# A grouped state-space recurrence: making the read matrices on GpSimd instead of VectorE

## The chip, the cores and the metric

One core of one Trainium2 chip. The metric is the device time of one launch of the whole kernel in microseconds. The kernel before takes 4410.57 us (median of 3 runs, 4408.84 to 4411.85).

## What is computed

Two transformer-like blocks over 256 tokens of width 2048, all in float32. The change touches one stage of the second block, the diagonal state-space layer of `layer_c`. Cut to what matters:

```python
def s5_ssm(u, lam_re, lam_im, log_step, b_re, b_im, c_re, c_im, d):
    """Groups of 16 channels share a 64-dim complex diagonal state.
    x_t = Lbar x_{t-1} + Bbar u_t ; y_t = Re(C x_t) + D u_t."""
    ...
    bu_re = jnp.einsum('gpc,blgc->blgp', bb_re, uf)
    bu_im = jnp.einsum('gpc,blgc->blgp', bb_im, uf)
    ...
    _, _, x_re, x_im = lax.associative_scan(_complex_combine, (a_re, a_im, bu_re, bu_im), axis=1)
    y = (jnp.einsum('gcp,blgp->blgc', c_re.astype(f32), x_re)
         - jnp.einsum('gcp,blgp->blgc', c_im.astype(f32), x_im))
    return y.reshape(Bsz, L, E) + d.astype(f32) * uf.reshape(Bsz, L, E)

def layer_c(x, ...):
    u, gate = jnp.split(h @ w_in, 2, axis=-1)
    y = s5_ssm(u, ...).astype(x.dtype)
    z = jax.nn.gelu(y)
    z = z * jax.nn.sigmoid(z @ glu_w + glu_b)
    return x + (z * jax.nn.silu(gate)) @ w_out
```

## The kernel before

The kernel is a row of stages with a barrier behind each. The stage in question is `s5_blocks` (line 1910), between the GEMM stage that makes `u` and the GEMM stage `glu`. Its 128 groups of channels are taken as 64 pairs (two groups of 64 states fill 128 partitions), and the 64 pairs in four batches `q` = 0 to 3 of 16 pairs (`QP`). Time is cut into steps of 4 tokens (`STEP`), and the 64 steps into 8 rows by 8 columns (`ROWS`, `COLS`). For each batch these pieces are made; the names are those of the functions in `s5_blocks`:

- **drive matrices** (GpSimd, lines 1962 to 1977). From the raw B coefficients (`ss_raw`) and a table of powers (`s_drive`): twice (real and imaginary part) a product into `ss_p`, a second product, and the sum or difference of both into `ss_drive_t`, in two halves of 64 partitions. 8 instructions a batch. `ss_drive_t` has one buffer, so batch q + 1 waits until TensorE has done `kernels(q)` (the wait on `within`, line 1966).
- **turn(q)** (TensorE) transposes them, ScalarE copies them out (`take_g`); **states(q)** multiplies them with `u`, ScalarE copies the result to `ss_x` (`take_x`).
- **read matrices** `read_rows(q)` (VectorE, lines 2105 to 2119). The same form from the raw C coefficients and the table `s_read`, for STEP + 1 = 5 powers: 8 instructions a batch, through `ss_b` into `ss_read`, which has two buffers. Its end counts up `h_done`, for which `kernels(q)` waits (line 2002). The SP queue's load of the raw coefficients of batch q + 2 waits for `gt_done` and `h_done` of batch q.
- **scan(q)** (VectorE, lines 2127 to 2139): the walk over the states in place in `ss_x`. 7 x 4 instructions of 128x256, one copy, 6 x 4 of 128x32, 7 x 4 of 128x256: 81 instructions, each waiting for the one before (`link`), then `scanned` counts up.
- **skip(q)** (VectorE, line 2144): one small product for the term D u; it waits for `kernels(q-1)`.
- **kernels(q)** (TensorE, lines 2009 and 2011): the matrices inside a step, from `ss_read` and `ss_drive_t`; ScalarE copies them to `ss_within` (`take_m`).
- **outputs(q)** (TensorE, lines 2023 and 2025): needs `take_m(q)` and `scan(q)` (line 2016); ScalarE puts the GELU of it into `c_ug` (`put`).

The orders are written by hand. TensorE: turn(0), states(0), kernels(0), then for each q: turn(q+1), states(q+1), outputs(q), kernels(q+1). ScalarE: take_u, take_g, take_x, take_m of batch q + 1, then put(q). VectorE: memsets of `ss_read`, `ss_within` and `ss_x`, skip(0), read_rows(0), then for each q: scan(q), skip(q+1), read_rows(q+1). GpSimd: a memset of `ss_drive_t`, then the drive matrices of the four batches.

Of the kernel before, what the change touches and what calls it, by code (L numbers as in the profile page):

```python
# [18 lines left out]
ALU = mybir.AluOpType  # L19
# [3 lines left out]
P = 128  # L23
# [1768 lines left out]
STEP = 4  # L1792
NQ = 4
QP = PAIRS // NQ
# [115 lines left out]
def s5_blocks(st, nc, t, banks, u, tables, con):  # L1910
# [3 lines left out]
    with ExitStack() as own, st.stage() as (block, sem):  # L1914
        def sb(name, shape):
            return own.enter_context(nc.sbuf_tensor("ss_" + name, shape, F32))

        drive, read, leaps = tables
        leap, leap_swing = leaps[:, ::2], leaps[:, 1:]
        C = 16  # L1920
        raw = sb("raw", [P, 2, QP, 4, C])
# [3 lines left out]
        h = sb("read", [P, 2, QP, 2, STEP + 1, 32])  # L1925
# [3 lines left out]
        b1, b2 = sb("b1", [P, QP, STEP + 1, C]), sb("b2", [P, QP, STEP + 1, C])  # L1929
# [3 lines left out]
        raw_in = [sem("ss_raw_in0"), sem("ss_raw_in1")]  # L1933
        d_in, cleared, zeroed, chain, gchain = sem("ss_d_in"), sem("ss_cleared"), sem("ss_zeroed"), sem("ss_chain"), sem("ss_gchain")
        gt_done, turned, g_out = sem("ss_gt_done"), sem("ss_turned"), sem("ss_g_out")
        h_done, within, m_out = sem("ss_h_done"), sem("ss_within"), sem("ss_m_out")
        stacked, driven, x_in = sem("ss_stacked"), sem("ss_driven"), sem("ss_x_in")
        scanned, y_done, z_out, d_done = sem("ss_scanned"), sem("ss_y_done"), sem("ss_z_out"), sem("ss_d_done")
        own_group = [(slice(64 * k, 64 * k + 64), slice(C * k, C * k + C)) for k in range(2)]
        stack = [(r, s) for r in range(4) for s in range(STEP)]  # L1940

        def pairs(q):
            return slice(q * QP, (q + 1) * QP)
# [4 lines left out]
        @block.sync  # L1948
        def _(sp):
            sp.dma_start(dcol[:, :], t["s5_d"]).then_inc(d_in, 16)  # L1950
            for q in range(NQ):
                if q >= 2:
                    sp.wait_ge(gt_done, 2 * (q - 1))
                    sp.wait_ge(h_done, 2 * (q - 1))
                sp.dma_start(raw[:, q % 2, :, :, :], t["s5_bc"][:, pairs(q), :, :]).then_inc(raw_in[q % 2], 16)

        @block.gpsimd
        def _(gp):
            link = Chain(gp, gchain)
            nc.gpsimd.memset(gt[:, :, :, :, :], 0.0).then_inc(cleared, 1)  # L1960
            gp.wait_ge(cleared, 1)
            for q in range(NQ):
                gp.wait_ge(raw_in[q % 2], 16 * (q // 2 + 1))
                if q >= 1:
                    gp.wait_ge(turned, 8 * q)
                    gp.wait_ge(within, 4 * q)
                row = lambda k: raw[:, q % 2, :, k, :].unsqueeze(2).broadcast_to([P, QP, STEP, C])
                by = lambda k: drive[:, k, :, pairs(q)].rearrange("p s q -> p q s").unsqueeze(3).broadcast_to([P, QP, STEP, C])
                for part, ((a, b), (c, d), op) in enumerate((((0, 0), (1, 1), ALU.subtract), ((0, 1), (1, 0), ALU.add))):
                    link(nc.gpsimd.tensor_tensor(p1[:, :, :, :], row(a), by(b), ALU.mult))  # L1970
                    link(nc.gpsimd.tensor_tensor(p2[:, :, :, :], row(c), by(d), ALU.mult))
                    for n, (rows, cols) in enumerate(own_group):
                        ins = nc.gpsimd.tensor_tensor(gt[rows, :, part, :, cols], p1[rows, :, :, :], p2[rows, :, :, :], op)
                        if n == 0:
                            link(ins)
                    ins.then_inc(gt_done, 1)
                    gp.wait_ge(gt_done, 2 * q + part + 1)

        @block.tensor
        def _(pe):  # L1980
# [115 lines left out]
        @block.vector  # L2096
        def _(dve):
            link = Chain(dve, chain)
            nc.vector.memset(h[:, :, :, :, :, :], 0.0).then_inc(zeroed, 1)
            nc.vector.memset(m[:, :, :, :], 0.0).then_inc(zeroed, 1)  # L2100
            nc.vector.memset(x[:, :, 0, :, :, 0], 0.0).then_inc(zeroed, 1)
            dve.wait_ge(d_in, 16)
            dve.wait_ge(zeroed, 3)

            def read_rows(q):
                dve.wait_ge(raw_in[q % 2], 16 * (q // 2 + 1))
                if q >= 2:
                    dve.wait_ge(y_done, 2 * (q - 1))
                row = lambda k: raw[:, q % 2, :, k, :].unsqueeze(2).broadcast_to([P, QP, STEP + 1, C])
                by = lambda k: read[:, k, :, pairs(q)].rearrange("p s q -> p q s").unsqueeze(3).broadcast_to([P, QP, STEP + 1, C])  # L2110
                for part, ((a, b), (c, d), op) in enumerate((((2, 0), (3, 1), ALU.subtract), ((2, 2), (3, 3), ALU.add))):
                    link(nc.vector.tensor_tensor(b1[:, :, :, :], row(a), by(b), ALU.mult))
                    link(nc.vector.tensor_tensor(b2[:, :, :, :], row(c), by(d), ALU.mult))
                    for n, (rows, cols) in enumerate(own_group):
                        ins = nc.vector.tensor_tensor(h[rows, q % 2, :, part, :, cols], b1[rows, :, :, :], b2[rows, :, :, :], op)
                        if n == 0:
                            link(ins)
                    ins.then_inc(h_done, 1)
                    dve.wait_ge(h_done, 2 * q + part + 1)

            def advance(out, previous, a, b, t1, t2):
                link(nc.vector.tensor_tensor(t1, previous, a, ALU.mult))
                link(nc.vector.tensor_tensor(t2, previous[:, ::-1], b, ALU.mult))
                link(nc.vector.tensor_tensor(t1, t1, t2, ALU.add))
                link(nc.vector.tensor_tensor(out, out, t1, ALU.add))

            def scan(q):
                xs = x[:, q % 2]
                dve.wait_ge(x_in, 4 * (q + 1))
                wide = lambda k: (leap[:, 0:1, k, pairs(q)].unsqueeze(3).broadcast_to([P, 2, QP, COLS]), leap_swing[:, :, k, pairs(q)].unsqueeze(3).broadcast_to([P, 2, QP, COLS]))  # L2130
                for i in range(1, ROWS):
                    advance(xs[:, i + 1], xs[:, i], *wide(0), m1[:, :, :, :], m2[:, :, :, :])
                link(nc.vector.tensor_copy(xs[:, 0, :, :, 1:], xs[:, ROWS, :, :, 0:COLS - 1]))
                for b in range(2, COLS):
                    advance(xs[:, 0, :, :, b], xs[:, 0, :, :, b - 1], leap[:, 0:1, ROWS - 1, pairs(q)].broadcast_to([P, 2, QP]), leap_swing[:, :, ROWS - 1, pairs(q)],
                            m1[:, :, :, 0], m2[:, :, :, 0])
                for i in range(1, ROWS):
                    advance(xs[:, i], xs[:, 0], *wide(i - 1), m1[:, :, :, :], m2[:, :, :, :])
                dve.sem_inc(scanned, 1)

            def skip(q):
                if q >= 1:
                    dve.wait_ge(within, 4 * q)
                nc.vector.tensor_tensor(diag[:, :, :], con["ident"][0:32, 0:32].unsqueeze(1).broadcast_to([32, QP, 32]),
                                        dcol[:, pairs(q)].unsqueeze(2).broadcast_to([32, QP, 32]), ALU.mult).then_inc(d_done, 1)

            skip(0)
            read_rows(0)
            for q in range(NQ):
                scan(q)  # L2150
                if q + 1 < NQ:
                    skip(q + 1)
                    read_rows(q + 1)


def layer_c(st, nc, t, banks, con, xT):

    with ExitStack() as own:
# [8 lines left out]
        with ExitStack() as s1:  # L2167
# [5 lines left out]
            def gate_out(act, f, psum, link):  # L2173
# [4 lines left out]
                dict(kind="fm", n=16, cols=T, rhs=lambda s, k: h[s][:, k, :], evac=gate_out)], gemm_buffers(sb, "c", s1, slots=2), banks,  # L2178
                operand=(h4, *h, quarters()))
        s5_blocks(st, nc, t, banks, ug[:, 0:KT, :], tables, con)  # L2180
        s5.close()
        buffers = gemm_buffers(sb, "c2", own)
# [322 lines left out]
```

## Time and profile before

| what | value |
|---|---|
| median of 3 runs | 4410.57 us |
| the profiled execution's own time | 4413.94 us |
| its span, first to last instruction | 4412.3 us |
| the stage s5_blocks in it | 3869.97 to 4170.06 us, 300.09 us |
| in the stage: PE, DVE, ACT, POOL busy | 183.45, 229.53, 148.02, 87.62 us |
| in the stage: mean granted TensorE clock | 0.69 |
| over the whole span: PE, DVE, ACT, POOL busy | 78%, 60%, 14%, 21% |

Instructions are named by their engine (PE is TensorE, PEld its weight loads, DVE VectorE, ACT ScalarE, POOL GpSimd) and by the line of the kernel. Busy times of a stretch say how much of it each engine worked; the granted clock is 1.00 at TensorE's full speed of 2.4 GHz and 0.50 at 1.2 GHz. Times in the rows are microseconds from the span's start.

### The profile page before, as it was taken

How to read it: one execution, taken by the hardware profiler on the slowest of the kernel's cores; microseconds unless marked ns; L12 is line 12 of the kernel's file. 1: busy time of each engine (PE TensorE's matmuls, PEld its weight loads, DVE VectorE, ACT ScalarE, POOL GpSimd, SP SyncE). 2: the span in 40 equal slices, each digit the busy share in tenths (PEclk: the TensorE clock that was granted, in tenths of full speed). 3: DMA queues.
4: the chain of work that ended last, by engine and by line, in shares of the span. 5: the costliest groups of instructions: out<-in, count | busy, mean ns of one | idle time of the engine just before them, and what ended most of it. 6: DMA issues, size and time to landing. Idle time of an engine off the chain costs nothing. (4 is left out here: it accounts for less than half of the span.)

```text
span 4412.3 us, 46250 instructions
## 1 busy us (share of the span) xinstructions
PE 3423.7 (78%) x17280; PEld 2498.0 (57%) x17280; DVE 2660.3 (60%) x3168; ACT 635.7 (14%) x1310; POOL 942.3 (21%) x753
## 2 busy tenths in 40 slices
PE   6899993776988755777778777779996687956688
PEld 1688671546988752333323333239874486944588
DVE  6774226657976567656566565426655466678665
ACT  0200002321100101111111111010003200134400
POOL 0100003002100016554545545300002000033040
PEclk9899895788989878999999999989996598976699
DMA  8573210025944439999999999935540033400143
GB/s 331 222 270 133 95 57 9 2 77 213 367 158 171 143 152 415 421 422 422 422 422 422 422 422 422 422 133 205 186 141 11 28 134 133 171 15 5 58 152 114
DMA packets 137329, 940.09 MB, mean 213 GB/s; under 512 B 17514, under 2 KB 22890, under 8 KB 24075
## 3 DMA queue, kind: packets, MB, share of 16 engines
q0 software_dynamic: 82944, 604.02, 33.5%
q1 hardware_dynamic: 54292, 334.89, 21.1%
q8 instruction: 52, 0.85, 0.1%
q14 instruction: 41, 0.34, 0.0%
HBM read 936.75 MB, written 2.10 MB: 213 GB/s over the span
## 5 line engine op out<-in xcount | busy, mean ns | idle before, releaser
L1313 PE MATMUL bank<-pe_v_rows,pe_diag 128*128 128x512 f32 x2048 | 959.8, 618 | 357.4 <-DMA pe_v_rows<-in_expert_v,pe_staged_v 215.2
L1313 PEld LDWEIGHTS bank<-pe_v_rows,pe_diag 128*128 128x128 f32 x2048 | 385.2, 196 | 931.4 <-issue 519.2
L1211 DVE SCALAR_TENSOR_TENSOR pe_junk<-pe_u_rows,h_rows 128x2048 f32<-128x2048 f32 x256 | 586.9, 2293 | 460.0 <-DMA pe_u_rows<-in_expert_u,pe_staged_u 448.9
L1155 POOL DMA_INDIRECT pe_v_rows<-in_expert_v,pe_staged_v x256 | 317.6, 1240 | 376.6 <-PE bank L1313 312.9
L1155 POOL DMA_INDIRECT pe_u_rows<-in_expert_u,pe_staged_u x256 | 338.0, 1320 | 228.3 <-DVE pe_junk L1211 134.4
L169 PE MATMUL bank<-h_top,b_top 128*128 128x256 f32 x1024 | 292.9, 286 | 40.2 <-DVE b_rest L237 40.2
L169 PE MATMUL bank<-h_rest,b_top 128*128 128x256 f32 x1024 | 292.3, 285 | 0.0
L169 PE MATMUL bank<-h_top,b_rest 128*128 128x256 f32 x1024 | 292.2, 285 | 0.0
L169 PEld LDWEIGHTS bank<-h_top,b_top 128*128 128x128 f32 x1024 | 199.4, 195 | 40.8 <-DVE b_rest L237 40.8
L1281 ACT ACTIVATE pe_diag<-ident,pe_weights 128x128 f32<-128x128 f32 x256 | 97.7, 399 | 786.9 <-PE bank L1313 786.5
L169 PEld LDWEIGHTS bank<-h_rest,b_top 128*128 128x128 f32 x1024 | 199.3, 195 | 0.0
L169 PEld LDWEIGHTS bank<-h_top,b_rest 128*128 128x128 f32 x1024 | 199.2, 195 | 0.0
L235 DVE CAST in_top<-in_ring 128x2048 fp32r<-128x2048 f32 x48 | 58.8, 1224 | 219.6 <-PE bank L195 134.6
L169 PE MATMUL bank<-h_top,in_top 128*128 128x256 f32 (+1 forms) x512 | 173.3, 339 | 11.2 <-DVE in_rest L237 11.2
L169 PE MATMUL bank<-h_rest,in_top 128*128 128x256 f32 (+1 forms) x512 | 173.1, 338 | 0.0
L169 PE MATMUL bank<-h_top,in_rest 128*128 128x256 f32 (+1 forms) x512 | 173.1, 338 | 0.0
L169 PE MATMUL bank<-gelu_top,c_top 128*128 128x256 f32 x512 | 147.3, 288 | 31.8 <-DVE c_rest L237 31.8
L169 PE MATMUL bank<-h_top,c_top 128*128 128x256 f32 x512 | 146.2, 286 | 20.8 <-DVE c_rest L237 20.8
L235 DVE CAST c_top<-c_ring 128x2048 fp32r<-128x2048 f32 x64 | 78.5, 1226 | 128.2 <-PE bank L169 128.2
L237 DVE TENSOR_TENSOR c_rest<-c_ring,c_top 128x2048 fp32r<-128x2048 f32 x64 | 150.9, 2358 | 2.2
L237 DVE TENSOR_TENSOR b_rest<-b_ring,b_top 128x2048 fp32r<-128x2048 f32 x64 | 146.7, 2292 | 2.2
L169 PE MATMUL bank<-gelu_rest,c_top 128*128 128x256 f32 x512 | 146.9, 287 | 0.0
(486 smaller groups left out, 7427.8 us busy)
## 6 DMA issues: line engine op xcount, KB each, us to landing
ab_ring<-in_w_ab SPq DMA_DIRECT2D x56, 1024.0 KB, 4.8
in_ring<-in_w_in_a SPq DMA_DIRECT2D x48, 1024.0 KB, 4.9
mod_ring<-in_w_mod SPq DMA_DIRECT2D x32, 1024.0 KB, 7.2
v_rows<-in_w_mod POOLq DMA_DIRECT2D x32, 1024.0 KB, 5.2
b_ring<-in_w_in_gates SPq DMA_DIRECT2D x32, 1024.0 KB, 5.2
k_cols<-in_w_mod POOLq DMA_DIRECT2D x32, 1024.0 KB, 5.3
c_ring<-in_w_c_in SPq DMA_DIRECT2D x32, 1024.0 KB, 4.8
b_ring<-in_w_branches SPq DMA_DIRECT2D x16, 1024.0 KB, 4.8
```

Of the source, the lines that this page charges most:

```text
L169: mm = nc.tensor.matmul(banks[s][:, half * n:(half + 1) * n], fast(weights), fast(seg["rhs"](b, k)), start=(j == 0 and m == 0), stop=(j == ...
L235: nc.vector.tensor_copy(fast(top[:, s % 2, :]), ring[:, s % slots, :]).then_inc(topped, 1)
L237: nc.vector.tensor_tensor(fast(rest[:, s % 2, :]), ring[:, s % slots, :], top[:, s % 2, :], ALU.subtract).then_inc(split_done, 1)
L1155: gp.indirect_dma_start(buf[:, slot, :], None, table, bass.IndirectOffsetOnAxis(ap=staged[which][:, tile, e:e + 1], axis=0)).then_inc(sems ...
L1211: nc.vector.scalar_tensor_tensor(out=junk[:, :], in0=ub[:, s, :], scalar=1.0, in1=h2tm[:, tile, :], op0=ALU.mult, op1=ALU.mult, accum_out= ...
L1281: nc.scalar.activation(diag[:, e % 4, :], con["ident"], ACT.Copy, scale=wts[:, tile, e:e + 1]).then_inc(diag_done, 1)
L1313: mm = nc.tensor.matmul(banks[4 * tile + b][:, :], diag[:, e % 4, :], vb[:, s, b * 512:(b + 1) * 512], start=False, stop=False, skip_group ...
```

## The change

Function `read_rows` moves from VectorE's program to GpSimd's, word for word but for the engine. GpSimd runs it for batch q right behind the drive matrices of batch q; its wait for VectorE's memsets (`zeroed`), which VectorE itself had, is made once, at q = 0. VectorE keeps the memsets, skip and scan. No size, buffer, load or semaphore count changes, and the programs of TensorE, ScalarE and the SP queue stay as they are. In the changed kernel the lines from here on have numbers that are 2 to 20 higher.

```diff
@@ GpSimd's program
             gp.wait_ge(cleared, 1)
+
+            def read_rows(q):
+                gp.wait_ge(raw_in[q % 2], 16 * (q // 2 + 1))
+                if q == 0:
+                    gp.wait_ge(zeroed, 3)
+                if q >= 2:
+                    gp.wait_ge(y_done, 2 * (q - 1))
+                row = lambda k: raw[:, q % 2, :, k, :].unsqueeze(2).broadcast_to([P, QP, STEP + 1, C])
+                by = lambda k: read[:, k, :, pairs(q)].rearrange("p s q -> p q s").unsqueeze(3).broadcast_to([P, QP, STEP + 1, C])
+                for part, ((a, b), (c, d), op) in enumerate((((2, 0), (3, 1), ALU.subtract), ((2, 2), (3, 3), ALU.add))):
+                    link(nc.gpsimd.tensor_tensor(b1[:, :, :, :], row(a), by(b), ALU.mult))
+                    link(nc.gpsimd.tensor_tensor(b2[:, :, :, :], row(c), by(d), ALU.mult))
+                    for n, (rows, cols) in enumerate(own_group):
+                        ins = nc.gpsimd.tensor_tensor(h[rows, q % 2, :, part, :, cols], b1[rows, :, :, :], b2[rows, :, :, :], op)
+                        if n == 0:
+                            link(ins)
+                    ins.then_inc(h_done, 1)
+                    gp.wait_ge(h_done, 2 * q + part + 1)
+
             for q in range(NQ):
                 gp.wait_ge(raw_in[q % 2], 16 * (q // 2 + 1))
...
                     ins.then_inc(gt_done, 1)
                     gp.wait_ge(gt_done, 2 * q + part + 1)
+                read_rows(q)
@@ VectorE's program
-            def read_rows(q):
...
             skip(0)
-            read_rows(0)
             for q in range(NQ):
                 scan(q)
                 if q + 1 < NQ:
                     skip(q + 1)
-                    read_rows(q + 1)
```

GpSimd's order of work from the first batch on, of the kernel before (`ss_drive_t` are the drive matrices; a batch is two such groups of three rows, and `x2` the two halves):

```order
L1960 MEMSET ss_drive_t 128x4096
L1970 TENSOR_TENSOR ss_p<-ss_raw,s_drive 128x1024
L1971 TENSOR_TENSOR ss_p<-ss_raw,s_drive 128x1024
L1973 TENSOR_TENSOR ss_drive_t<-ss_p 64x16x4x16 x2
L1970 TENSOR_TENSOR ss_p<-ss_raw,s_drive 128x1024
L1971 TENSOR_TENSOR ss_p<-ss_raw,s_drive 128x1024
L1973 TENSOR_TENSOR ss_drive_t<-ss_p 64x16x4x16 x2
L1970 TENSOR_TENSOR ss_p<-ss_raw,s_drive 128x1024
```

The same place of the changed kernel (lines 1989 to 1992 are the drive matrices there, 1972 to 1975 the read matrices):

```order
L1989 TENSOR_TENSOR ss_p<-ss_raw,s_drive 128x1024
L1990 TENSOR_TENSOR ss_p<-ss_raw,s_drive 128x1024
L1992 TENSOR_TENSOR ss_drive_t<-ss_p 64x16x4x16 x2
L1972 TENSOR_TENSOR ss_b<-ss_raw,s_read 128x1280
L1973 TENSOR_TENSOR ss_b<-ss_raw,s_read 128x1280
L1975 TENSOR_TENSOR ss_read<-ss_b 64x16x5x16 x2
L1972 TENSOR_TENSOR ss_b<-ss_raw,s_read 128x1280
L1973 TENSOR_TENSOR ss_b<-ss_raw,s_read 128x1280
L1975 TENSOR_TENSOR ss_read<-ss_b 64x16x5x16 x2
L1989 TENSOR_TENSOR ss_p<-ss_raw,s_drive 128x1024
```

Between the drive matrices of two batches, 8 instructions of 1280 elements a partition now stand in GpSimd's queue.

VectorE's order at the end of a scan, of the kernel before:

```order
L2125 TENSOR_TENSOR ss_x<-ss_x,ss_m 128x256
L2144 TENSOR_TENSOR ss_skip<-ident,ss_d 32x512
L2112 TENSOR_TENSOR ss_b<-ss_raw,s_read 128x1280
L2113 TENSOR_TENSOR ss_b<-ss_raw,s_read 128x1280
L2115 TENSOR_TENSOR ss_read<-ss_b 64x16x5x16 x2
```

and of the changed kernel:

```order
L2129 TENSOR_TENSOR ss_x<-ss_x,ss_m 128x256
L2148 TENSOR_TENSOR ss_skip<-ident,ss_d 32x512
L2126 TENSOR_TENSOR ss_m<-ss_x,s_leaps 128x256
L2127 TENSOR_TENSOR ss_m<-ss_x,s_leaps 128x256
L2128 TENSOR_TENSOR ss_m<-ss_m 128x256
```

The next scan follows right behind skip.

## Rows read from the trace of the kernel before

**Rows 1.** Busy time by engine, the whole stage (us, count; then clock, DMA share, GB/s)

```profile
3869.97:4170.06 300.09, 183.45 (x1152) 145.54 (x1152) 229.53 (x363) 148.02 (x321) 87.62 (x33) 0.69 0.02 8
```

**Rows 2.** Waits in the stage: who waited for whom, us, times, longest

```profile
POOL ss_p L1970 <- PE bank L2011: 128.5, 3, 61.8
...
PE bank L1987 <- POOL ss_drive_t L1973: 93.0, 4, 27.9
```

**Rows 3.** Timeline of TensorE: start, us, work, count, idle time before it

```profile
3943.48 1.75 PE L1987 MATMUL bank<-ident,ss_drive_t 128*128 128x128 f32 x7 [18.21 <-POOL ss_drive_t L1973]
...
3960.13 0.41 PE L2023 MATMUL bank<-ss_u,ss_within 128*128 128x64 f32 x2 [3.09 <-DVEq L2139]
...
3980.16 1.06 PE L2009 MATMUL bank<-ss_read,ss_drive_t 128*32 128x128 f32 x4
...
4046.03 0.39 PE L2023 MATMUL bank<-ss_u,ss_within 128*128 128x64 f32 x2
...
4056.85 0.62 PE L2009 MATMUL bank<-ss_read,ss_drive_t 128*32 128x128 f32 x4
...
4109.29 0.39 PE L2023 MATMUL bank<-ss_u,ss_within 128*128 128x64 f32 x2
...
4142.84 0.66 PE L2023 MATMUL bank<-ss_u,ss_within 128*128 128x64 f32 x2 [8.51 <-ACT c_ug L2082]
```

**Rows 4.** Busy time by engine, three stretches of outputs and kernels (clock behind POOL's)

```profile
3960.13:4005.10 44.97, 44.95 (x192) 31.37 (x192) 41.71 (x90) 5.11 (x12) 0.00 (x0) 0.51 0.04 12
4046.03:4071.10 25.07, 25.05 (x194) 18.56 (x193) 21.95 (x64) 5.77 (x14) 0.00 (x0) 1.00 0.01 1
4142.84:4163.00 20.16, 20.16 (x95) 20.16 (x95) 0.00 (x0) 12.15 (x32) 0.00 (x0) 0.50 0.00 1
```

**Rows 5.** Timeline of GpSimd, drive matrices of three batches

```profile
3875.09 2.01 POOL L1970 TENSOR_TENSOR ss_p<-ss_raw,s_drive 128x1024 f32<-128x1024 f32 x1 [1.63 <-DMA ss_raw<-in_s_bc]
...
3925.45 2.01 POOL L1970 TENSOR_TENSOR ss_p<-ss_raw,s_drive 128x1024 f32<-128x1024 f32 x1 [28.40 <-PE bank L2011]
...
3929.63 4.78 POOL L1973 TENSOR_TENSOR ss_drive_t<-ss_p 64x1024 f32<-64x1024 f32 x2
...
4071.25 2.30 POOL L1970 TENSOR_TENSOR ss_p<-ss_raw,s_drive 128x1024 f32<-128x1024 f32 x1 [38.30 <-PE bank L2011]
4073.63 2.07 POOL L1971 TENSOR_TENSOR ss_p<-ss_raw,s_drive 128x1024 f32<-128x1024 f32 x1
4075.78 4.88 POOL L1973 TENSOR_TENSOR ss_drive_t<-ss_p 64x1024 f32<-64x1024 f32 x2
```

**Rows 6.** Timeline of VectorE, parts of three scans

```profile
3929.66 2.40 DVE L2122 TENSOR_TENSOR ss_m<-ss_x,s_leaps 128x32 f32<-128x32 f32 x1
...
3972.86 0.42 DVE L2122 TENSOR_TENSOR ss_m<-ss_x,s_leaps 128x256 f32<-128x256 f32 x1
...
3985.70 0.28 DVE L2133 COPY ss_x<-ss_x 128x224 f32<-128x224 f32 x1
...
3992.04 0.43 DVE L2122 TENSOR_TENSOR ss_m<-ss_x,s_leaps 128x256 f32<-128x256 f32 x1
...
4073.86 2.12 DVE L2123 TENSOR_TENSOR ss_m<-ss_x,s_leaps 128x256 f32<-128x256 f32 x1
4076.02 2.45 DVE L2124 TENSOR_TENSOR ss_m<-ss_m 128x256 f32<-128x256 f32 x1
...
4110.25 0.43 DVE L2122 TENSOR_TENSOR ss_m<-ss_x,s_leaps 128x256 f32<-128x256 f32 x1 [3.45 <-ACT ss_x L2063]
```

**Rows 7.** Timeline of VectorE, half of the read matrices of a batch

```profile
4094.67 1.47 DVE L2112 TENSOR_TENSOR ss_b<-ss_raw,s_read 128x1280 f32<-128x1280 f32 x1
...
4097.70 3.01 DVE L2115 TENSOR_TENSOR ss_read<-ss_b 64x1280 f32<-64x1280 f32 x2
```

**Rows 8.** Timeline of GpSimd, dense two-input products elsewhere in the kernel

```profile
1021.95 6.42 POOL L990 TENSOR_TENSOR o_a<-o_a,mo_wa 128x2048 f32<-128x2048 f32 x1
...
3500.14 4.51 POOL L1724 TENSOR_TENSOR ab_of<-ab_of,ab_gates 128x2048 f32<-128x2048 f32 x1 [99.15 <-POOLq L51]
```

More of the change, by code:

```diff
@@ L2103, in _ @@
             dve.wait_ge(zeroed, 3)
-            def read_rows(q):
[L2106 to L2119, printed above, removed]
             def advance(out, previous, a, b, t1, t2):
```

## Prediction

> **What bounds the kernel now.** The change touches one stage of 300.09 us, so I read that stretch by itself. First the busy times [rows 1]: no engine is full; VectorE works 229.53 us of it, TensorE 183.45, GpSimd only 87.62. Going by shares, moving work from VectorE to GpSimd looks right. The waits say something else [rows 2]: GpSimd waits 128.5 us in all for TensorE's kernels, and TensorE waits 93.0 us for GpSimd's drive matrices. The stage is a ring: kernels(q) end, drive matrices(q+1), turn and states(q+1), outputs(q), kernels(q+1). I call the end of kernels(q) K(q). Before, K(0) is 3925.3 (GpSimd starts again at 3925.45 [rows 5]), K(1) 4005.1, K(2) 4071.1 [rows 4].
>
> Two things disturb the ring. **The clock** [rows 3, 4]: outputs and kernels took 25.07 us where they followed states at once (granted clock 1.00), and 44.97 us after a pause of 3.09 us (0.51). After a pause of 8.51 us outputs alone took 20.2 us at 0.50, against 4056.85 - 4046.03 = 10.8. Slow kernels alone are 4005.10 - 3980.16 = 24.9 us. 1.00 is 2.4 GHz and 0.50 is 1.2. **VectorE and GpSimd block each other**: a walk instruction of 128x256 takes 0.46 us from start to start (28 of them and nothing else fill 3972.86 to 3985.70), but while drive matrices are made it takes 2.12 or 2.45 us, as long as the GpSimd instruction beside it (2.07, and 4.88 for two); even one of 128x32 takes 2.40 us [rows 5, 6]. So while GpSimd works through two-input instructions, VectorE gets one of its own in for each. GpSimd hardly suffers: 2.07 against 2.01.
>
> **What is moved, and its price.** VectorE gives up 8 instructions a batch, half a batch from 4094.67 to 4100.7 [rows 7], 12.1 us a batch. GpSimd gains them. It has no such instruction of 1280 elements; the nearest are its own drive instructions of 1024 in the same layout. Two products and their gaps are 4.18 us, two halves 4.86 with the gap [rows 5], so drive matrices take 2 x 9.04 = 18.1 us. Scaled by 1280/1024, half a batch of read matrices is 5.2 + 6.1 = 11.3 and a batch 22.6 us. Bounds: below, no growth with size, 18.1; above, the dense products of 2048 elements, 4.51 us (2.8 for 1280), and far off 6.42 (4.0) [rows 8], up to some 33 us a batch. I take 22.6, the same form.
> - Where does it lie? Behind the drive matrices, beside turn and states. GpSimd's chain for a batch is now 18.1 + 22.6 = 40.7 us from K(q), some 42 when VectorE takes turns with it. TensorE needs 18.8 + 13.6 (turn and states, 3943.48 to 3957.04) + 10.8 (outputs) = 43.2 before it wants `ss_read`. From batch 1 on read matrices are on time.
> - The cost is on scan(q). It needs 3 parts: 12.8 + 6.3 + 12.8 = 32 us alone [rows 6]. It now meets 16 GpSimd instructions a batch instead of 8, and moves 16 steps of its 81 in those 42 us.
> - Waits added on GpSimd: `zeroed` is long there, `y_done` is two batches old. The load of the raw coefficients leaves later but is needed a batch later; nothing. The 8 matching waits go from VectorE; its skip is 0.7 us as before.
>
> The Trainium skill, page SBUF — State Buffer, section "two separate sides", calls the shared ports an exclusive lock held for the whole instruction, the loser fully blocked. The rows agree on VectorE's side; on GpSimd's, 2.07 against 2.01 with a 0.42 us instruction between says most of that one is hidden. By the rule each GpSimd instruction in contention would be 0.4 us longer, and the sum some 6 us more (16 of them in scan(1)'s way).
>
> **The walk.** Drive(0) starts at 3875.09 and is no longer disturbed by read rows on VectorE: it ends at 3875.09 + 18.1 + 0.2 for skip(0) = 3893.4. States(0) end at 3907.0. Read(0) ends at 3916.0, so kernels(0) start after a pause of 9.0 us, at half clock like the 8.51 us pause: K(0) = 3916.0 + 24.9 = 3940.9, 15.6 later than before. Scan(0) starts 1 us behind states [rows 3, 6], at 3908.0. It gets 3 steps in until 3916.0, then 24.9 us free: 25 large, the copy, 24 small, 15 large. 13 are left at K(0): 8 beside drive(1), 5 beside read(1), done at K(0) + 18.9 + 14.2 = 33.1. States(1) end at K(0) + 32.5. No pause worth the name, so outputs(0) and kernels(1) run fast: K(1) = K(0) + 58.2 = 3999.1. Before it was 79.8: this turn gains 21.6.
>
> Scan(1) starts at K(0) + 33.9, does 3 steps until 42.0 and in the free 16.2 us about 43; 35 are left at K(1). 16 go by until K(1) + 42.0, 19 more in 8.7: done at 50.7. States(2) end at K(1) + 38.2, as now from K(2) to 4109.29 (ScalarE is first busy with put and take_u). TensorE pauses 12.5 us and outputs(1) and kernels(2) run at half clock, 45.0: K(2) = K(1) + 95.8 = 4094.9, against 66.0 before. Scan(2) then finds GpSimd idle and is done before K(2), so the third turn stays at 63. Scan(3) starts at about K(2) + 39 as before, with one or two of its steps held up by the end of read(3), and what follows stays: 0 to 1.5 us. Sum against the profiled execution: +15.6 - 21.6 + 29.8 + 0.7 = **+24.5 us**, all in this stage. That execution took 4413.94 by its own time; the median of the runs is 4410.57, 0.08% below. Forecast 4410.57 + 24.5 = **4435**. A difference of 0.2%, 8.8 us, is about what a measurement of this kernel can tell from none.
>
> **Rivals.**
> - *One step more in scan(0)* (chance 0.17). The tie of 33.1 against 32.5 is the walk's weakest place. One more blocked step, 3 us, makes a pause like the 3.09 us one: outputs(0), kernels(1) slow, K(1) = K(0) + 81. Then scan(1) is in time (K(2) = K(1) + 63.3 = 4085.2), scan(2) ends at K(2) + 45.2, K(3) comes 90.3 behind K(2), and the last outputs follow at half clock, 35.5 us (8 for the first half of put(2), 20.2, and 7 from 4163.0 to 4170.06 as now): end at 4211, +41, 4451.
> - *GpSimd's instructions nearer the dense bound* (0.10): 2.8 and 3.3 us instead of 2.5 and 3.0. Read(0) ends 2.6 later and each contended scan pays again: 4446; at 4.0 us about +60.
> - *The clock comes back while TensorE works* (0.11). K(0) = 3930.3; scan(0) ends at K(0) + 53, K(1) near 4008.4, K(2) 4075.3, scan(3) at K(2) + 74.6. With fast last outputs the end is 1.5 us before today's, with slow ones 7 behind: 4409 to 4418. Against it: 45 us of busy TensorE in [rows 4] at 0.51. The Trainium skill, TensorE: Matmul & The Clock Gate, Part 1, has sustained activity release the throttle; by that rule this is the case. Here transposes got the clock back and outputs and kernels did not.
> - *Faster: the ring gains because scans keep up* (0.06). If GpSimd's 1280 instructions cost no more than those of 1024 (read batch 18.1 us), or the two engines did not block each other, scan(1) ends by K(1) + 40, too little pause for the clock to fall: K(1) 3993 to 3998, K(2) near 4060, then 99 us: end 10 to 13 before today's, 4398 to 4401. It decides where a read batch is under about 20 us. For it: VectorE does lose 12.1 us a batch. Against it: [rows 5, 6].
>
> **The numbers.** The forecast case has 0.56, with small variations of 4 to 5 us in K(0) and scan(1). Faster 0.06, same 0.11 (the clock rival), slower 0.83. The range 4412 to 4452 holds the forecast case, the tie rival, the upper part of the clock rival and most of the dense one; left out are the faster case, the low edge of the clock rival and the far bound of GpSimd's price, under 2 in 10.
>
> **What would show it.** Read instructions on GpSimd near 2.5 and 3.0 us; VectorE's walk instructions of 2 to 3 us beside them, some 16 a batch; kernels(0) starting near 3916 after a pause, clock 0.50; K(0) near 3941, K(1) near 3999, K(2) near 4095; outputs(1) waiting for scan(1) by 10 us or more at half clock; the stage about 325 us long. Wrong if walk instructions keep 0.46 us beside the new ones, if the clock returns within kernels(0), or if the stage is not longer than 309 us.

## The result and the profile after

The changed kernel takes 4440.28 us (median of 6 runs, 4432.85 to 4449.17) against 4411.74 (6 runs, 4408.84 to 4415.32) of the kernel before: 1.0066 times as long, 95% interval 1.0053 to 1.0079, +28.5 us. Forecast was 4435, in a range of 4412 to 4452. Run again on another occasion (5 runs, against 13 of the kernel before) it was 4438.82 against 4414.94, 1.0053 times (1.0039 to 1.0067), +23.9.

| | before | after |
|---|---|---|
| the profiled execution's own time | 4413.94 | 4449.17 |
| its span | 4412.3 | 4447.1 |
| stage s5_blocks | 3869.97 to 4170.06, 300.09 | 3881.26 to 4205.10, 323.84 |
| in the stage: PE, DVE, ACT, POOL busy | 183.45, 229.53, 148.02, 87.62 | 196.19, 209.12, 148.21, 162.18 |
| in the stage: granted clock | 0.69 | 0.64 |

The stage grew by 23.75 us; forecast +24.5. In this execution the stages ahead of it, whose code is the same, took another 11.3 us (the stage begins at 3881.26 instead of 3869.97). In the second profiled execution of the same program the stage began at 3862.70, earlier than before, and again took 323.85. So the stage's length belongs to the program, and the 11.3 us ahead of it are scatter of an execution.

Busy time by engine of the changed kernel over the stage, as in [rows 1]:

```profile
3881.26:4205.10 323.84, 196.19 (x1152) 150.96 (x1152) 209.12 (x331) 148.21 (x321) 162.18 (x65) 0.64 0.02 7
```

GpSimd's busy time has nearly doubled. VectorE's fell by only 20 us, although its read instructions had been busy for 66 us before (35.3 + 17.0 + 13.9 in the groups by shape): blocked steps count as busy. The waits in the stage (who waited for whom, us, times, longest), as in [rows 2]:

```profile
POOL ss_p L1989 <- PE bank L2031: 95.9, 3, 55.4
...
PE bank L2007 <- POOL ss_drive_t L1992: 80.1, 4, 24.4
DVE ss_m L2126 <- ACT ss_x L2083: 60.0, 2, 38.5
```

VectorE now waits 60.0 us for the states, 27.1 before: it has time to spare in some batches and none in others. Timeline of TensorE, the first matmuls behind its pauses (idle time in brackets), and outputs(0), which follow states without one:

```profile
3927.03 1.06 PE L2029 MATMUL bank<-ss_read,ss_drive_t 128*32 128x128 f32 x4 [8.19 <-POOL ss_read L1975]
...
3984.20 0.39 PE L2043 MATMUL bank<-ss_u,ss_within 128*128 128x64 f32 x2
...
4059.60 0.66 PE L2043 MATMUL bank<-ss_u,ss_within 128*128 128x64 f32 x2 [10.79 <-issue]
...
4177.88 0.66 PE L2043 MATMUL bank<-ss_u,ss_within 128*128 128x64 f32 x2 [9.38 <-DVEq L2143]
```

Busy times of the four stretches of kernels and outputs that begin there, the clock third from the end:

```profile
3927.03:3952.00 24.97, 24.92 (x96) 11.39 (x96) 22.74 (x66) 5.13 (x13) 0.00 (x0) 0.50 0.07 22
3984.10:4009.30 25.20, 25.15 (x195) 18.66 (x194) 23.73 (x45) 5.79 (x15) 9.64 (x4) 1.00 0.07 22
4059.50:4105.20 45.70, 45.57 (x192) 31.96 (x192) 29.87 (x82) 5.12 (x12) 0.00 (x0) 0.50 0.00 1
4177.88:4198.60 20.72, 20.71 (x96) 20.52 (x96) 0.00 (x0) 11.35 (x30) 0.00 (x0) 0.50 0.00 1
```

Kernels(0) at half clock after a pause of 8.19 us; outputs(0) and kernels(1) at full clock, 25.2 us, where they took 44.97 before [rows 4]; outputs(1) and kernels(2) at half clock, 45.7, after 10.79.

Added up along TensorE, the 23.75 us are these. Half clock adds 41.0 us to what the same matmuls take at 1.00, against 29.7 before: 10.7 in kernels(0), 20.5 in outputs(1) and kernels(2), 9.8 in outputs(3). That is 11.3 more. The pauses ahead of kernels and outputs are 28.4 us, against 11.6: 16.8 more. Turn(0) starts 23.6 us into the stage and not 27.1, 3.6 less, since VectorE's read matrices no longer hold up the drive matrices of batch 0. The rest is 0.8 less.

Timeline of GpSimd from K(0) on, drive matrices and then read matrices (as [rows 5]):

```profile
3952.12 2.22 POOL L1989 TENSOR_TENSOR ss_p<-ss_raw,s_drive 128x1024 f32<-128x1024 f32 x1 [25.15 <-PE bank L2031]
...
3956.57 4.91 POOL L1992 TENSOR_TENSOR ss_drive_t<-ss_p 64x1024 f32<-64x1024 f32 x2
...
3970.83 2.54 POOL L1972 TENSOR_TENSOR ss_b<-ss_raw,s_read 128x1280 f32<-128x1280 f32 x1
...
3976.09 5.99 POOL L1975 TENSOR_TENSOR ss_read<-ss_b 64x1280 f32<-64x1280 f32 x2
```

and of VectorE's walk at the same time (as [rows 6]):

```profile
3952.50 2.12 DVE L2126 TENSOR_TENSOR ss_m<-ss_x,s_leaps 128x256 f32<-128x256 f32 x1
...
3956.81 2.46 DVE L2128 TENSOR_TENSOR ss_m<-ss_m 128x256 f32<-128x256 f32 x1
...
3971.07 2.59 DVE L2126 TENSOR_TENSOR ss_m<-ss_x,s_leaps 128x256 f32<-128x256 f32 x1
...
3976.32 3.00 DVE L2128 TENSOR_TENSOR ss_m<-ss_m 128x256 f32<-128x256 f32 x1
```

Each step lasts about as long as the GpSimd instruction it meets: 2.12 and 2.46 beside drive matrices, 2.59 and 3.00 beside read matrices, against 0.42 alone.

### The profile page after: what moved, and what is told of

It reads as the page before. It is cut to its first block and busy times, and to the rows that moved or that the text cites. A ratio compares the mean times of both kernels' runs of the same rounds, so it can differ in the third digit from the quotient of the medians.

```text
span 4447.1 us, 46248 instructions
## 1 busy us (share of the span) xinstructions
PE 3450.2 (78%) x17280; PEld 2512.5 (56%) x17280; DVE 2640.7 (59%) x3136; ACT 636.0 (14%) x1310; POOL 1028.1 (23%) x785
## 5 line engine op out<-in xcount | busy, mean ns | idle before, releaser
L169 PE MATMUL bank<-h_top,in_top 128*128 128x256 f32 (+1 forms) x512 | 173.2, 338 | 11.3 <-DVE in_rest L237 11.3
```

Source lines behind the costliest of these rows:

```text
L169: mm = nc.tensor.matmul(banks[s][:, half * n:(half + 1) * n], fast(weights), fast(seg["rhs"](b, k)), start=(j == 0 and m == 0), stop=(j == ...
```

## The experiments

Theory A is the prediction's: the two engines block each other, scans come late or in time according to how much free time the batch before left them, and TensorE's clock halves in a pause. Rival B: GpSimd is simply slower, and only matrices that come late cost. Rival C: late scans are the loss, the clock goes along.

**The changed kernel again**, nothing edited.

> The changed kernel once more. Theory A (VectorE's walk steps and GpSimd's two-input instructions block each other, and TensorE's clock halves in the pauses this makes): the stage s5_blocks takes 324 us within 3, with the same four ends of kernels, and the whole kernel 4435 to 4445. In the first profile the stages ahead, whose code is the same, took 11.3 us more than before: if that was scatter of one execution, a new profile shows less of it and the median comes nearer to +24; if it belongs to this program, it comes again.

4438.82 us against 4414.94 before (interval above). The stage took 323.85 us, and the four ends of kernels, counted from the stage's start, are the same within 0.2 us: 70.6, 128.0, 224.0, 287.3. The stages ahead did not repeat their 11 us. The two gaps between medians, +28.5 and +23.9, differ by less than their intervals allow.

**Only batch 0 moved.**

```diff
@@ GpSimd
-                read_rows(q)
+                if q in (0,):
+                    read_rows(q)
@@ VectorE
+                    if q + 1 not in (0,):
+                        read_rows(q + 1)
```

> Only batch 0's read matrices on GpSimd, batches 1 to 3 on VectorE. Theory A: kernels(0) still start late and at half clock (K(0) 15.6 us later than before), which gives scan(0) time to get on, so scan(0) is done when states(1) end, outputs(0) and kernels(1) run at full clock and K(1) = K(0) + 57.6; after that no scan meets read matrices on GpSimd, K(2) = K(1) + 63.3, and the stage ends 9 us EARLIER than before: 4402, between 4399 and 4409. Rival B (GpSimd is just the slower engine, and read matrices that come late are the whole loss): all of the loss is at kernels(0), so this kernel keeps it, +15 us: 4426.

4405.22 us, 0.9976 times the kernel before (0.9966 to 0.9986): faster by 9.7 us. The stage took 291.63 us, 8.5 less. Timeline of TensorE: kernels(0) behind their pause, and outputs(0) without one; and the clock of outputs(0) and kernels(1):

```profile
3913.17 1.06 PE L2030 MATMUL bank<-ss_read,ss_drive_t 128*32 128x128 f32 x4 [8.22 <-POOL ss_read L1975]
...
3970.35 0.39 PE L2044 MATMUL bank<-ss_u,ss_within 128*128 128x64 f32 x2
```

```profile
3970.30:3995.40 25.10, 25.10 (x194) 18.61 (x193) 22.91 (x65) 5.77 (x14) 0.00 (x0) 1.00 0.07 22
```

The late and slow kernels(0) are all there, and the kernel gains. The time they cost is what scan(0) needs to be done before states(1), and 25.1 us at full clock take the place of 44.97. Rival B, which keeps +15 us, falls.

**Only batches 1 to 3 moved.** The same edit with `(1, 2, 3)`; VectorE makes batch 0.

> Batch 0's read matrices on VectorE as before, batches 1 to 3 on GpSimd. Theory A: K(0) as before (3925), but scan(0) has moved only 29 steps by then and needs until K(0) + 57, so outputs(0) and kernels(1) run at half clock, K(1) = K(0) + 102; K(2) = K(1) + 63; scan(2) is late again by 7 us, K(3) = K(2) + 90: the stage ends 46 us later than before, 4457, between 4440 and 4465, slower than the changed kernel although less was moved. Rival B: the matrices of batches 1 to 3 are in time for kernels, so 4412, as before.

4456.25 us, 1.0092 times (1.0076 to 1.0107). Less is moved than in the changed kernel and it is slower. The stage took 344.15 us, 44 more than before (46 worked out). Timeline of TensorE at outputs(0), and the busy times from there:

```profile
3975.90 0.66 PE L2044 MATMUL bank<-ss_u,ss_within 128*128 128x64 f32 x2 [23.29 <-DVEq L2160]
```

```profile
3976.00:4021.00 45.00, 45.00 (x191) 31.87 (x192) 29.75 (x82) 5.11 (x12) 0.00 (x0) 0.50 0.00 1
```

TensorE waited 23.29 us for scan(0), then ran 45 us at half clock. Kernels(1), (2) and (3) followed outputs without a pause, so all read matrices were in time, and rival B's 4412 falls.

**Work that nobody waits for.**

```diff
@@ GpSimd, behind the drive matrices of each batch of the kernel before
+                for part in range(2):
+                    for _ in range(2):
+                        link(nc.gpsimd.tensor_tensor(p1[:, :, :, :], p1[:, :, :, :], p2[:, :, :, :], ALU.subtract))
+                    for rows, cols in own_group:
+                        link(nc.gpsimd.tensor_tensor(p1[rows, :, :, :], p1[rows, :, :, :], p2[rows, :, :, :], ALU.subtract))
```

> The kernel before, with 8 more two-input GpSimd instructions of 1024 elements behind each batch's drive matrices, whose results nobody reads and nobody waits for; GpSimd is idle there. VectorE keeps its read matrices. Theory A: scans lose 8 more of their steps' time per batch and VectorE's chain of a batch gets longer, outputs(0) run late and slow: +20 to +50 us, 4432 to 4462. Rival B (only the matrices' lateness costs): no one waits for these, 4412 within 4.

4462.49 us, 1.0106 times (1.0091 to 1.0122), +47.6, 0.5 us above the upper end of what was expected; the stage took 352.0 us. The new instructions delay no matrix of GpSimd's: ahead of each further batch it still waited for kernels (15.49, 55.43 and 19.09 us). What they hold up is VectorE. Timeline of TensorE at kernels(0) and at outputs(0):

```profile
3907.76 1.06 PE L2014 MATMUL bank<-ss_read,ss_drive_t 128*32 128x128 f32 x4 [1.73 <-DVE ss_read L2120]
...
3980.41 0.66 PE L2028 MATMUL bank<-ss_u,ss_within 128*128 128x64 f32 x2 [15.93 <-DVEq L2144]
```

First VectorE's read matrices of batch 0 come late; kernels(0) run at half clock behind a pause of 1.73 us and end 67.8 us into the stage instead of 55.3. Then scan(0) is late, and TensorE pauses 15.93 us ahead of outputs(0). So the loss is the blocking and the half clock behind it, and rival B falls.

**The pauses filled.**

```diff
@@ TensorE
+            def keep_busy(n):
+                for _ in range(n):
+                    nc.tensor.transpose(banks[0][:, 0:P], con["ident"], con["ident"])
             turn(0)
             states(0)
+            keep_busy(37)
             kernels(0)
...
+                keep_busy((95, 13, 13, 34)[q])
                 outputs(q)
```

> The changed kernel, with transposes of the identity into a bank that nobody reads put where TensorE would pause: 37 ahead of kernels(0), 95 ahead of outputs(0), 13 ahead of outputs(1) and (2), 34 ahead of outputs(3), each about as long as the pause that I work out at full clock. Theory A with the clock as a separate part: kernels(0), outputs and kernels all run at 1.00; scan(0) then meets the read matrices with 42 steps left and ends at K(0) + 53, K(1) = K(0) + 78, K(2) and K(3) 67 apart, stage 299 us within 5, whole kernel 4409 to 4418: most of the change's loss was the half clock. Rival C (lateness of the scans is the loss, the clock only goes along): the stage stays at 320 or more, 4435.

4423.52 us, 1.0025 times (1.0014 to 1.0037), above the 4418 that was the upper end. The profile says why. Timeline of TensorE at kernels(0), of this kernel:

```profile
3900.42 4.21 PE L2051 MATMUL bank<-ident 128*128 128x128 f32 x37
3908.84 0.89 PE L2029 MATMUL bank<-ss_read,ss_drive_t 128*32 128x128 f32 x4 [4.22 <-POOL ss_read L1975]
```

37 transposes lasted 4.21 us, 0.114 each; I had taken 0.21 from those of turn, which wait on ScalarE. A pause of 4.22 us stayed open and kernels(0) took 24.8 us again. The stage took 324.00 us in this execution, no less than in the changed kernel. It was one of the longer ones, 4431.12 us; the ten runs lie between 4417.21 and 4437.47. That the others had fewer stretches at half clock is likely, but not shown, since only this one was profiled. It settles nothing about C, so it was repeated with 72, and 180, 30, 30, 70:

> moved_busy with enough filling: in its trace the transposes went by every 0.114 us, not 0.21, and left half of each pause open (4.2 us ahead of kernels(0)), so that the clock still fell. Now 72 ahead of kernels(0), 180 ahead of outputs(0), 30 ahead of outputs(1) and (2), 70 ahead of outputs(3). Theory A with the clock as a separate part: no kernels or outputs at half clock, K(1) = K(0) + 78, K(2) and K(3) 67 apart, stage 299 us within 6, whole kernel 4410 to 4418. Rival C (late scans are the loss, the clock goes along): 4423 or more.

4414.93 us, 0.9998 times (0.9989 to 1.0007): as the kernel before. Busy times of kernels(0), and of outputs(0) with kernels(1):

```profile
3915.30:3929.60 14.30, 14.22 (x96) 7.80 (x96) 13.10 (x36) 5.15 (x13) 0.00 (x0) 1.00 0.13 38
3982.30:4007.50 25.20, 25.06 (x192) 18.60 (x192) 22.99 (x66) 5.15 (x13) 0.00 (x0) 1.00 0.00 1
```

Both at full clock. The distances of the kernels' ends are 77.9, 67.6 and 66.9 us, worked out 78, 67, 67. The stage took 304.39 us, 19.5 less than the changed kernel's: so much goes when the clock is held, though scan(0) ends later than in either kernel (113 us into the stage; 101 in the changed kernel, 90 before). Rival C as it is stated, 4423 or more, falls. 304.39 stays above the 299 worked out: in the second half of outputs(3) the clock fell all the same (10.05 us, the first half 5.54).

**The same filling in the kernel before**, 14 ahead of outputs(0) and 50 ahead of outputs(3).

> The kernel before, with 14 such transposes ahead of outputs(0) (its pause of 3.09 us) and 50 ahead of outputs(3). Theory A: outputs(0) and kernels(1) take 25 us instead of 45, outputs(3) 11 instead of 21; the later batches shift but stay without pauses; the stage gets 28 us shorter, 272, whole kernel 4387, between 4380 and 4400. Rival C: 4415 as before.

4402.23 us, 0.9973 times (0.9964 to 0.9983), less than half of the gain worked out, in part from the same wrong 0.21 us. The stage took 290.74 us in the profiled execution, one of the longer ones (4408.81; the ten runs lie between 4395.94 and 4409.39). Outputs(0) ran fast, but the pauses were only partly closed and a new one came, since kernels(1) now wait for VectorE's read matrices. Timeline of TensorE, and the busy times behind the second pause:

```profile
3965.14 0.41 PE L2023 MATMUL bank<-ss_u,ss_within 128*128 128x64 f32 x2 [1.70 <-DVEq L2145]
...
3977.89 0.62 PE L2009 MATMUL bank<-ss_read,ss_drive_t 128*32 128x128 f32 x4 [1.85 <-DVE ss_read L2121]
```

```profile
3985.00:4000.00 15.00, 15.00 (x60) 6.81 (x58) 13.50 (x45) 3.44 (x9) 0.00 (x0) 0.50 0.00 0
```

Kernels(1) fell to half clock after pauses of 1.70 and 1.85 us with 11 us of work between. I had not listed this wait: with outputs(0) fast, VectorE's 12.1 us of read matrices stand on the path.

Held clocks shorten both kernels. So these two experiments show that half clock is a cost of its own in each, but not that it is most of what the change costs, as the expectation above says. With transposes in both kernels, the stage is still some 14 us longer with the read matrices on GpSimd (304.39 against 290.74), and neither has its clock held throughout. By the sum along TensorE above, pauses have the larger share.

**The opposite move.**

```diff
@@ VectorE
+            def drive_rows(q):
...
+            drive_rows(0)
             skip(0)
             read_rows(0)
             for q in range(NQ):
                 scan(q)
                 if q + 1 < NQ:
+                    drive_rows(q + 1)
                     skip(q + 1)
                     read_rows(q + 1)
@@ GpSimd: the drive matrices go, two memsets of VectorE's come
+            nc.gpsimd.memset(h[:, :, :, :, :, :], 0.0).then_inc(zeroed, 1)
+            nc.gpsimd.memset(m[:, :, :, :], 0.0).then_inc(zeroed, 1)
```

> The opposite move: VectorE makes the drive matrices too (8 instructions of 1024 elements, 1.25 us each, behind scan(q)), and GpSimd only the memsets of ss_drive_t, ss_read and ss_within. No two-input instruction of GpSimd is left to block VectorE. Theory A: VectorE's instructions all keep their own length (0.42, 1.2, 1.5 us), a batch costs it 32 + 10 + 12 = 54 us, and the stage takes 275 us within 5, whole kernel 4390. Rival B (VectorE is the busiest engine of the stage, 77% by its busy time, and more work on it must lengthen it): 40 us more work, 4440 or so.

4388.15 us, 0.9942 times (0.9926 to 0.9959). The stage took 275.05 us. Timeline of VectorE in this kernel behind scan(0), drive matrices and then read matrices:

```profile
3933.32 1.23 DVE L2094 TENSOR_TENSOR ss_p<-ss_raw,s_drive 128x1024 f32<-128x1024 f32 x1 [0.26 <-DVE ss_x L2123]
...
3935.84 2.47 DVE L2097 TENSOR_TENSOR ss_drive_t<-ss_p 64x1024 f32<-64x1024 f32 x2
...
3943.98 1.47 DVE L2110 TENSOR_TENSOR ss_b<-ss_raw,s_read 128x1280 f32<-128x1280 f32 x1
```

Every instruction keeps its own length. The drive matrices of a batch cost VectorE 10.1 us here. On GpSimd they took 18, in which the walk got only 8 of its steps done, 3.7 us of its work. VectorE has more instructions, is busy for 206.41 us instead of 229.53, since none of them is blocked, and the stage is 25 us shorter. Half of that is at the start: kernels(0) end 43.0 us into the stage instead of 55.3, since the matrices of batch 0 are no longer made by two engines that block each other. The two memsets that go to GpSimd have a part in this, which was not tried by itself. The other half is K(0) to K(1), 67.8 us instead of 79.8, with outputs(0) and kernels(1) at full clock.

**GpSimd with one input.** In the changed kernel, products and sums of the read matrices replaced by copies of the same size.

```diff
-                    link(nc.gpsimd.tensor_tensor(b1[:, :, :, :], row(a), by(b), ALU.mult))
-                    link(nc.gpsimd.tensor_tensor(b2[:, :, :, :], row(c), by(d), ALU.mult))
+                    link(nc.gpsimd.tensor_copy(b1[:, :, :, :], row(a)))
+                    link(nc.gpsimd.tensor_copy(b2[:, :, :, :], row(c)))
```

> The changed kernel with its 32 read instructions on GpSimd turned into one-input copies of the same size (the products and sums of the read matrices are left out). If only two-input GpSimd instructions block VectorE, its walk steps beside the copies last 0.46 us; if any GpSimd instruction that reads SBUF blocks it, each step beside a copy lasts as long as the copy. I expect the second, with copies of 1.2 to 1.8 us, and the stage shorter than the changed one by 10 us or more.

One run, 4414.19 us; the stage took 304.81. Timeline of GpSimd and of VectorE at the same time:

```profile
3936.20 1.25 POOL L1972 COPY ss_b<-ss_raw 128x1280 f32<-128x1280 f32 x1
```

```profile
3936.24 1.28 DVE L2128 TENSOR_TENSOR ss_m<-ss_m 128x32 f32<-128x32 f32 x1
```

A walk step of 0.22 us lasts 1.28 beside a copy of 1.25, so a second input of GpSimd's instruction is not needed. That GpSimd must read is shown by the opposite move: there its memsets, which only write, ran beside VectorE's drive matrices of batch 0. Timelines of GpSimd and of VectorE in that kernel:

```profile
3874.83 8.63 POOL L1960 MEMSET ss_read<- 128x10240 f32 x1
```

```profile
3877.84 1.22 DVE L2095 TENSOR_TENSOR ss_p<-ss_raw,s_drive 128x1024 f32<-128x1024 f32 x1
```

VectorE's product kept its 1.22 us. The Trainium skill, SBUF — State Buffer, section "two separate sides", says that a VectorE instruction with two SBUF inputs contends with a GpSimd instruction that reads SBUF and not with one that only writes; the rows agree.

**The best of them.** The opposite move, with 72 transposes ahead of outputs(3).

> all_on_vectore with 72 transposes in the one pause of TensorE that a half clock follows, ahead of outputs(3) (8.5 us): outputs(3) take 11 instead of 20.7 us and the stage 260 instead of 269, whole kernel 4379 (4374 to 4388), below both kernels of this study. If the clock falls in spite of the filling: 4388.

4378.52 us, 0.9918 times the kernel before (0.9905 to 0.9932), the fastest here. The stage took 270.77 us, 4.3 less than without the filling; the 269 in what was expected was a misreading of 275.05. Each against the kernel before as run beside it, this kernel gains 38.0 us and the one without the filling 26.0, 12 us apart. The stages of the two profiled executions show 4.3 of them; where the rest lies is not known. Busy times in outputs(3):

```profile
4111.00:4114.00 3.00, 2.68 (x24) 2.71 (x25) 0.01 (x1) 2.83 (x8) 0.00 (x0) 1.00 0.00 0
...
4117.00:4120.00 3.00, 2.20 (x12) 2.20 (x12) 0.00 (x0) 2.83 (x8) 0.00 (x0) 0.67 0.02 5
4120.00:4124.00 4.00, 4.00 (x20) 4.00 (x21) 0.00 (x0) 3.76 (x11) 0.00 (x0) 0.50 0.00 0
```

The first half ran at full clock and the second fell: outputs(3) pause once more in their middle for ScalarE (0.94 us), which the filling does not cover.

## Why the prediction was right

- **The price of a read instruction.** 2.48 and 2.9 us, forecast 2.5 and 3.0; a batch 22.1 us (3904.85 to 3926.98), forecast 22.6. GpSimd's chain of a batch was 41.9 us from K(0), forecast 42. Without VectorE beside it, in batch 0, it was 40.4, so taking turns cost GpSimd 1.5 us and not the 6 that the prediction worked out as an alternative. VectorE got one instruction in for each of GpSimd's 16, with one exception: a step of 0.40 us slipped in behind skip(1), beside a GpSimd product that took 3.14 us.
- **Kernels(0) late and slow.** Pause 8.19 (9.0 forecast), clock 0.50, K(0) 15.4 us later from the stage's start (15.6).
- **Scan(0) just in time.** This was the weak place, with scan(0) ending 33.1 us behind K(0) and states(1) 32.5. It ended at K(0) + 30.4, with 12 steps left at K(0) instead of 13, and outputs(0) started at K(0) + 32.2. The order that the forecast rests on, scan(0) within a step of states(1), was too close to be foreseen from the rows, and that it fell on this side was in part luck; as measured, one step more would have made a pause of 1.2 us and two one of 4.2. K(0) to K(1) was 57.3 us, forecast 58.2.
- **Scan(1) late.** It ended 50.2 us behind K(1), forecast 50.7. K(1) to K(2) was 95.9, forecast 95.8. States(2) took until K(1) + 39.6, not 38.2, so the pause was 10.8 and not 12.5. The row of this pause names no engine; scan(1) ended at 4059.43 and outputs(1) started at 4059.60.
- **The rest.** From K(2) to the stage's end 99.9 us, forecast 99 to 100.5.
- The clock rival is refuted: 24.97 and 45.7 us of busy TensorE stayed at 0.50. The Trainium skill, TensorE: Matmul & The Clock Gate, Part 1, lets sustained activity release the throttle; these two stretches do not show it. The faster rival is refuted for this kernel, but its mechanism (scans keep up, so the clock does) is what made the kernel with only batch 0 moved faster.
- The sum was 0.75 us above the stage's growth. The medians, +28.5 and +23.9, differ from it by up to 4 us for which no step in the stage is to blame. The whole kernel's time scatters by more than that: 16 us over 6 runs of the changed kernel, and 15.5 over the 13 later runs of the kernel before.
- What I had not priced, and met only in the experiments: a transpose without waits (0.114 us), and the wait of kernels for VectorE's read matrices once outputs run fast.

## What to carry to other kernels

Before moving two-input work from VectorE to GpSimd, add up both engines' instructions that read SBUF as if they were one engine's, with GpSimd's at their longer time: here a batch went from 32 + 12 + 18 to 32 + 22 + 18 us, and moving all of it the other way gave 54 and the faster kernel. Such a sum ranks these three kernels (62, 72 and 54). It does not give the time of a batch, which was 70, 72 and 65 us on average from K(0) to K(3). Busy shares hide this, since a blocked step counts as busy. Where TensorE has pauses, ask of each delay which pause it opens or closes: the same slow kernels(0) came with a loss in one version and a gain in another.

## What was not expected of the hardware

- The length of a short pause does not tell by itself whether the clock falls. Ahead of outputs(0), pauses of 1.14 us (72 and 180 transposes) and of 1.70 us (the kernel before with 14) left the clock at 1.00 through all 10.9 us of outputs(0). In the latter, a pause of 1.85 us behind them brought kernels(1) to half clock within about 2 us. With 8 more GpSimd instructions, kernels(0) behind a pause of 1.73 us ran at 0.50 from their start.
- TensorE stayed at half clock through 45 us without a gap in outputs and kernels (45.0 us at 0.51, 45.7 at 0.50). In the kernel before, turn(2) started at 4033.01 after a further 28 us of pause, at 0.50, and about 3 us into its transposes, from 4036 on, the clock was 1.00. The 256-column matmuls of the next stage did the same in about 5 us (start 4181.43, 0.50 until 4186 and 1.00 from 4187 on).
- GpSimd's copies of 1280 elements take 1.25 us, half of its two-input instructions (2.48), and still hold up a VectorE step of 0.22 us for their whole length, while GpSimd itself loses 0.06 to 0.1 us beside a short step.
- Beside long VectorE instructions GpSimd loses as much. The prediction's "hardly suffers" holds for walk steps alone. Timelines of GpSimd and of VectorE in the kernel before, drive matrices and read matrices of batch 0 at the same time:

```profile
3890.04 7.01 POOL L1973 TENSOR_TENSOR ss_drive_t<-ss_p 64x1024 f32<-64x1024 f32 x2
```

```profile
3891.34 7.06 DVE L2115 TENSOR_TENSOR ss_read<-ss_b 64x1280 f32<-64x1280 f32 x2
```

Undisturbed, the same two instructions take 4.77 us on GpSimd (start 3879.28) and 3.01 on VectorE [rows 7].
